# Token gathers of an expert-choice layer: two halves of eight experts, or eight pairs

## Chip, cores and metric

The kernel runs on one core of one Trainium2 chip. The metric is the time of one execution on the device, in microseconds (us). Three runs of the kernel before gave 1915.8, 1917.1 and 1922.41 us; their median is 1917.1 us.

## What is computed

The reference is a chain of two transformer blocks. The first has two layers (a gated linear attention with sparse attention, then pooling with stick-breaking attention, each with a gated feed-forward network). The second puts 16 meta tokens ahead of the 256 tokens (272 rows of 1024 features), runs differential attention and a convolution, and ends with the expert layer, which is the part that matters here:

```python
def expert_choice_ffn(h, w_router, w_gate, w_up, w_down):
    cap = EC_CAPACITY_FACTOR * L // N_EXPERTS        # 2 * 272 // 16 = 34
    def one_group(hs):
        aff = jax.nn.softmax(jnp.einsum('ld,de->le', hs, w_router), axis=-1)
        g, idx = lax.top_k(aff.T, cap)
        xg = hs[idx]
        a = jnp.einsum('ecd,edf->ecf', xg, w_gate)
        u = jnp.einsum('ecd,edf->ecf', xg, w_up)
        y = jnp.einsum('ecf,efd->ecd', jax.nn.silu(a) * u, w_down)
        y = y * g[..., None]
        return jnp.zeros((L, D)).at[idx.reshape(-1)].add(y.reshape(-1, D))
```

Each of 16 experts picks the 34 tokens with the highest affinity to it, runs them through gate, up and down matrices (1024 by 2048, 1024 by 2048, 2048 by 1024, all float32), and its weighted outputs are added back to the tokens' rows. Every expert has its own 24 MiB of weights, 384 MiB in all.

## The kernel before, in words

Every engine has a program of its own, written out by hand; all waits are on semaphores. The parts of the program follow one another: first layer, its feed-forward part, second layer, its feed-forward part, differential attention, experts (`pe_experts`, `act_experts`, `dve_experts`, `pool_experts`, and the tail of `sync_program`).

**Routing.** `pe_experts` multiplies by the router (line 919), turns the logits, the affinities and the tokens (lines 925, 940, 933), and counts the rank of each picked token (line 956). VectorE finds the picks with five rounds of eight maxima (lines 2067 and 2069), and writes the one-hot matrix `OH` (line 2089): for each token row, 16 experts by 34 places, a one where the token takes that place of that expert. It is written for experts 0 to 7 first, and then for 8 to 15, in three instructions each, one for each tile of token rows (128, 128 and 16 rows). The semaphore `onehot` counts them.

**Gather.** The tokens' rows are gathered by matmuls (line 969). The tokens `FT` are the stationary operand (128 features of one token tile), `OH` the moving one. For each of 8 feature chunks and each half of the experts, three matmuls (token tiles of 128, 128 and 16 rows) add up in one PSUM bank, 272 columns wide (8 experts by 34). ScalarE copies the odd chunks to `XG`, VectorE the even ones (line 2096). A float32 matmul stands as two MATMUL records and two LDWEIGHTS records in the trace, so the 24 matmuls of a half are 48 records. The first half is gathered in front of expert 0, the second in two portions of four chunks, behind the first gate/up step of experts 2 and 3.

**An expert.** Gate and up are done in four steps of 512 columns each (`gate_up(e, i)`, lines 990 and 991, 16 matmuls in a step; the gate uses the array's columns 0 to 33, and the up matmul beside it columns 64 to 97). ScalarE applies the silu (line 1473), VectorE multiplies (line 2104), TensorE turns the result (`turn_hidden`, line 1000), and four steps `down(e, i)` follow (lines 1011 and 1012). Behind `gate_up(e, 0)` other work is put: the gather portions at e = 2 and 3, two turns of the way back for each e from 1 to 4 (`back_map`, line 977), and at each even e from 2 the addition of the last pair of experts to the tokens (`combine`, line 1027).

**Weights.** SyncE starts all weight transfers in order, 2 MiB each, into a ring of five slots (`sp_weight`, line 2261). For each expert the order is g0 u0 g1 u1 g2 u2 g3 u3 d0 d1 d2 d3. A transfer into a slot is issued when the TensorE step that read the slot last has ended. `gate_up` frees two slots at its end, and `down` one. At the end of `gate_up(e, 0)` the transfers of g1, u1 and g2 have been issued already, and u2 and g3 follow; at the end of `gate_up(e, 1)` come u3 and d0. Expert 0 is different: its g0, u0, g1, u1 and g2 are loaded into the ring during the attention, and u2, g3 and u3 into places outside the ring (lines 2333 and 2339) during the routing. The next transfer, d0 of expert 0, needs the slots of `gate_up(0, 0)`.

**PSUM.** The eight banks are used in turn in the order of the TensorE program (`pe_bank`); a use waits until the last reader of the use before has taken it.

Of the kernel before, what the change touches and what calls it, by code (L numbers as in the profile page):

```python
# [16 lines left out]
KC = D // 128  # L17
# [7 lines left out]
E_N = 16  # L25
CAP = 2 * L // E_N
# [2 lines left out]
NHD = 6  # L29
MAGIC = 12582912.0  # L30
NP = 64 + CAP
LAM0 = 0.8 - 0.6 * math.exp(0.0)
TILES = ((0, 128), (128, 128), (256, 16))
SET_EXP, SET_SILU, SET_SIN = 6, 18, 9
# [370 lines left out]
def pe_bank(nc, k, key, takers=1, hold=False):  # L405
    u = k.banks.take(key, takers, hold)
    if u.before:
        nc.tensor.wait_ge(u.taken, u.before)
    return u
# [502 lines left out]
def pe_experts(nc, k):  # L912
    pe, s, v, P, ring = nc.tensor, k.sem, k.ex, k.banks, k.ring
    ident, ones = k.cc("ident"), k.cc("ones")
    u = pe_bank(nc, k, "router")
    pe.wait_ge(s["small"], 16)
    for c in range(KC):
        pe.wait_ge(s["hn"], HN["ffn2"] + c + 1)
        ins = pe.matmul(u.t[0:16, 0:L], k.WS[:, c, :], k.H[:, c, :], start=c == 0, stop=c == KC - 1)
    ins.then_inc(u.full, 1)  # L920
    u = pe_bank(nc, k, "route", takers=2)
    t = P["router"]
    pe.wait_ge(t.taken, t.done)
    for i, (r, m) in enumerate(TILES):
        ins = pe.transpose(u.v(3, 16)[0:m, i, :], v.LG[0:16, r:r + m], ident[0:16, 0:16])
# [11 lines left out]
    u = pe_bank(nc, k, "affinity")  # L937
    for i, (r, m) in enumerate(TILES):
        pe.wait_ge(s["raff"], 2 * i + 2)
        ins = pe.transpose(u.t[0:16, r:r + m], v.AFF[0:m, i, :], ident[0:m, 0:m])  # L940
# [3 lines left out]
    u = pe_bank(nc, k, "picked")  # L944
    pe.wait_ge(s["rtop"], 10)
    for i, (r, m) in enumerate(TILES):
        ins = pe.transpose(u.v(3, 16)[0:m, i, :], v.WK[0:16, 6 + r:6 + r + m], ident[0:16, 0:16])
    ins.then_inc(u.full, 1)
    u = pe_bank(nc, k, "rank")
    t = P["picked"]  # L950
    pe.wait_ge(t.taken, t.done)
    for i, (r, m) in enumerate(TILES):
        for j in range(i + 1):
            km = TILES[j][1]
            lt = k.cc("before")[0:km, 0:m] if j == i else ones[0:km, 0:m]
            ins = pe.matmul(u.v(3, 16)[0:m, i, :], lt, v.MSK[0:km, j, :], start=j == 0, stop=j == i)
    ins.then_inc(u.full, 1)
    for i in range(3):
        for half in range(2):
            t = P["tokens", i, half]  # L960
            pe.wait_ge(t.taken, t.done)
    hw = E_N * CAP // 2

    def gather(half, c):
        u = pe_bank(nc, k, ("gather", half, c))
        for i, (r, m) in enumerate(TILES):
            if c == 0:
                pe.wait_ge(s["onehot"], 3 * half + i + 1)
            ins = pe.matmul(u.t[:, 0:hw], v.FT[0:m, i, c * 128:(c + 1) * 128], v.OH[0:m, i, half * hw:(half + 1) * hw],  # L969
                            start=i == 0, stop=i == 2)  # L970
        ins.then_inc(u.full, 1)

    def back_map(g):
        u = pe_bank(nc, k, ("back", g))
# [5 lines left out]
    def gate_up(e, i):  # L980
        wg, wu = k.gate_up_at(e, i)
        u = pe_bank(nc, k, ("egu", e, i))
        pe.wait_ge(wg.sem, wg.n)
        pe.wait_ge(wu.sem, wu.n)
        for c in range(KC):
            if i == 0 and e % 8 == 0:
                t = P["gather", e // 8, c]
                pe.wait_ge(t.taken, t.done)
            xs = v.XG[:, c, e * CAP:(e + 1) * CAP]
            pe.matmul(u.t[0:CAP, :], xs, wg.v(KC, 512)[:, c, :], start=c == 0, stop=c == KC - 1)  # L990
            ins = pe.matmul(u.t[64:64 + CAP, :], xs, wu.v(KC, 512)[:, c, :], start=c == 0, stop=c == KC - 1)  # L991
        ins.then_inc(u.full, 1)
        wg.left = wu.left = (u.full, u.n)
# [32 lines left out]
                stat.upto(max(c - 3, 0))  # L1026
            pe.matmul(u.t[:, 0:L], v.Y[0:NP, g % 2, c * 128:(c + 1) * 128], v.OGT[0:NP, g, :], start=True, stop=True).then_inc(u.full, 1)  # L1027

    for c in range(KC):
        gather(0, c)  # L1030
    for e in range(E_N):
        gate_up(e, 0)
        if e in (2, 3):
            for c in range(4 * e - 8, 4 * e - 4):
                gather(1, c)
        if 1 <= e <= 4:
            back_map(2 * e - 2)
            back_map(2 * e - 1)
        if e and e % 2 == 0:
            combine(e // 2 - 1)  # L1040
        gate_up(e, 1)
        turn_hidden(e, 0)
        gate_up(e, 2)
        turn_hidden(e, 1)
        gate_up(e, 3)
        turn_hidden(e, 2)
        u = pe_bank(nc, k, ("eo", e), takers=2, hold=True)
        down(e, 0, u)
        turn_hidden(e, 3)
        for i in range(1, 4):  # L1050
            down(e, i, u)
        P.drop(("eo", e))
# [17 lines left out]
def act_table(nc, n):  # L1070
    nc.scalar.add_instruction(mybir.InstLoadActFuncSet(
        name=nc.get_next_instruction_name(), engine=mybir.EngineType.Activation, act_func_set_id=n, ins=[], outs=[]))


def act_out(nc, u, dst, src, f=ACT.Copy, **kw):

    nc.scalar.wait_ge(u.full, u.n)
    nc.scalar.activation(dst, src, f, **kw).then_inc(u.taken, 1)
# [365 lines left out]
def act_experts(nc, k):  # L1444
    act, s, v, P = nc.scalar, k.sem, k.ex, k.banks
    act_stat(nc, k, "ffn2", 0)
    act_out(nc, P["router"], v.LG[0:16, :], P["router"].t[0:16, 0:L])
    u = P["route"]
    act.wait_ge(u.taken, u.done - 1)
    for i, (r, m) in enumerate(TILES):  # L1450
        act.activation(v.AFF[0:m, i, :], u.v(3, 16)[0:m, i, :], ACT.Exp, bias=v.mx[0:m, i:i + 1],
                       accum_out=v.sm[0:m, i:i + 1]).then_inc(s["rexp"] if i < 2 else u.taken, 1)

    def turn_tokens(i):
        m = TILES[i][1]
        for half in range(2):
            act_out(nc, P["tokens", i, half], v.FT[0:m, i, half * 512:half * 512 + 512], P["tokens", i, half].t[0:m, :])

    for i in range(3):
        turn_tokens(i)  # L1460
    hw = E_N * CAP // 2

    def gather(half, c):
        if c % 2:
            act_out(nc, P["gather", half, c], v.XG[:, c, half * hw:(half + 1) * hw], P["gather", half, c].t[:, 0:hw])

    def gate(e, i):
        u = P["egu", e, i]
        act.wait_ge(u.full, u.n)
        if 4 * e + i >= 2:  # L1470
            t = P["egu", e, i - 2] if i >= 2 else P["egu", e - 1, i + 2]
            act.wait_ge(t.taken, t.done)
        act.activation(v.SG[0:CAP, i % 2, :], u.t[0:CAP, :], ACT.Silu).then_inc(s["esilu"], 1)  # L1473

    for c in range(KC):
        gather(0, c)
    act_table(nc, SET_SILU)
    for e in range(E_N):
        gate(e, 0)
        if e in (2, 3):  # L1480
            for c in range(4 * e - 8, 4 * e - 4):
                gather(1, c)
        if 1 <= e <= 4:
            for g in (2 * e - 2, 2 * e - 1):
                act_out(nc, P["back", g], v.OGT[0:NP, g, :], P["back", g].t[0:NP, 0:L])
        for i in range(1, 4):
            gate(e, i)
        u, g, r = P["eo", e], e // 2, 64 * (e % 2)
        act.wait_ge(u.full, u.n)
        if e == 0:  # L1490
            act.wait_ge(s["yzero"], 1)
        if g >= 2:
            t = P["comb", g - 2, KC - 1]
            act.wait_ge(t.full, t.n)
        act.activation(v.Y[r:r + CAP, g % 2, 0:512], u.t[0:CAP, :], ACT.Copy).then_inc(u.taken, 1)
        act.activation(v.Y[r:r + CAP, g % 2, 512:1024], u.t[64:64 + CAP, :], ACT.Copy).then_inc(u.taken, 1)
    for c in range(KC):
        act_square(nc, k, M, c, P["comb", 7, c])
    act_table(nc, SET_EXP)
    act_stat(nc, k, "fin", M)  # L1500
# [542 lines left out]
def dve_experts(nc, k):  # L2043
# [30 lines left out]
    t, u = u, P["rank"]  # L2074
    dve.wait_ge(u.full, u.n)
    dve.wait_ge(t.taken, t.done)
    for half in range(2):
        for i, (r, m) in enumerate(TILES):
            if not half:
                dve.scalar_tensor_tensor(out=v.SV[0:m, i, :], in0=u.v(3, 16)[0:m, i, :], scalar=1.0, in1=v.MSK[0:m, i, :],  # L2080
                                         op0=ALU.add, op1=ALU.mult).then_inc(s["rank"] if i < 2 else u.taken, 1)
                if i < 2:
                    dve.wait_ge(s["rank"], i + 1)
                else:
                    dve.wait_ge(u.taken, u.done)
            o = v.OH[0:m, i, half * 8 * CAP:(half + 1) * 8 * CAP].rearrange("p (e s) -> p e s", s=CAP)
            io = k.cc("iota")[0:m, :].rearrange("p (a s) -> p a s", a=1).to_broadcast([m, 8, CAP])
            sv = v.SV[0:m, i, 8 * half:8 * half + 8].rearrange("p (e a) -> p e a", a=1).to_broadcast([m, 8, CAP])
            dve.tensor_tensor(o, io, sv, ALU.is_equal).then_inc(s["onehot"], 1)
    hw = E_N * CAP // 2  # L2090

    def gather(half, c):
        if c % 2 == 0:
            u = P["gather", half, c]
            dve.wait_ge(u.full, u.n)
            dve.tensor_copy(v.XG[:, c, half * hw:(half + 1) * hw], u.t[:, 0:hw]).then_inc(u.taken, 1)

    def hidden(e, i):
        u, n = P["egu", e, i], 4 * e + i
# [20 lines left out]
                dve.wait_ge(t.taken, t.done)  # L2120
            dve_residual(nc, k, u, u.t[:, 0:L], c, 0, None)

    for c in range(KC):
        gather(0, c)
    for e in range(E_N):
        hidden(e, 0)
        if e in (2, 3):
            for c in range(4 * e - 8, 4 * e - 4):
                gather(1, c)
        if e and e % 2 == 0:  # L2130
            combine(e // 2 - 1)
        hidden(e, 1)
        turned(e, 0)
        hidden(e, 2)
        turned(e, 1)
        hidden(e, 3)
        turned(e, 2)
        turned(e, 3)
# [337 lines left out]
```

## Time and profile before

| | |
|---|---|
| median of 3 runs | 1917.1 us |
| the profiled execution, its own time | 1914.45 us |
| its span in the profile | 1912.8 us |
| TensorE busy | 1672.8 us (87%), 8723 matmul records |
| VectorE, ScalarE, GpSimd busy | 33%, 20%, 3% |
| moved by DMA | 577.30 MB, mean 302 GB/s |
| mean granted TensorE clock | 0.941 of full speed |
| chain that ended last | TensorE 67%, DMA 24%, VectorE 6% |
| gate/up matmuls of line 990 | 1008 records, busy 483.6 us; idle ahead of them 128.2 us, ended by the DMA of the up weights |

The routing ends and the gather begins 941 us after the start of the span; the experts run from 967 to 1896 us. A row of the stage table has the time window, its length, for each engine the busy us and the number of instructions, then the granted TensorE clock (1.00 is 2.4 GHz, 0.50 is 1.2 GHz), the busy share of the DMA engines and the rate in GB/s. A row of a timeline has start, duration from the start of the first to the end of the last instruction merged, engine, line, and in square brackets the idle time before it with what ended it.

### The profile page before, as it was taken

The page shows a single profiled execution, that of the slowest core. Times are in us where ns is not written, and L with a number is a line of the kernel's source. Part 1 is how long each engine was busy: PE and PEld are TensorE (multiplying, and loading weights), DVE is VectorE, ACT ScalarE, POOL GpSimd, SP SyncE. Part 2 cuts the span into 40 slices and gives each one's busy share as a digit, 9 for nine tenths or more (in the row PEclk, how much of TensorE's full clock was granted, in tenths as well). Part 3 has the DMA queues.
Part 4 walks back from the last instruction along what each step waited for, and adds up shares of the span by engine and source line. Part 5 has one row for each costly group of instructions (what it writes and reads, how often), then busy time and mean ns, then how long its engine had stood idle before and what let it go on. Part 6 is the DMA issues. An engine that isn't in the chain of part 4 may idle for free.

```text
span 1912.8 us, 20481 instructions
## 1 busy us (share of the span) xinstructions
PE 1672.8 (87%) x8723; PEld 998.9 (52%) x8723; DVE 634.1 (33%) x1218; ACT 378.8 (20%) x659; POOL 51.0 (3%) x47
## 2 busy tenths in 40 slices
PE   2998899999889998999798888978879788888787
PEld 1775799997679998767432322322223222222223
DVE  5567277745847554352310100101001010010102
ACT  3213344333333433141100000000000000000001
POOL 4101000000000000100010000000000000000000
PEclk7989999999989999999789999989999899899999
DMA  9554258646547445223459899999999999999995
GB/s 398 217 220 179 107 199 331 240 155 246 223 173 265 166 168 197 88 88 131 177 224 424 367 428 404 429 430 427 430 431 430 431 430 431 430 424 429 428 430 242
DMA packets 43740, 577.30 MB, mean 302 GB/s; under 512 B 4721, under 2 KB 6786, under 8 KB 7298
## 3 DMA queue, kind: packets, MB, share of 16 engines
q1 hardware_dynamic: 43650, 576.00, 73.4%
q8 instruction: 69, 1.13, 0.2%
q14 instruction: 21, 0.17, 0.0%
HBM read 574.93 MB, written 1.05 MB: 301 GB/s over the span
## 4 chain that ended last, share of the span: by engine, by line
PE 67%; DMA 24%; DVE 6%; ACT 2%; issue 1%; POOL 1%; SPq 0%; DVEq 0%; ACTq 0%
DMA RING_T<-in_w_up 22%; PE P L990 16%; PE P L419 13%; PE P L1011 6%; PE P L700 4%; PE P L701 4%; PE P L702 4%; PE P L428 3%; PE P L721 2%; PE P L720 2%; PE P L719 2%; PE P L969 2%; PE P L1027 2%; DVE RING_T L1565 1%; DMA RING_T<-in_ada_w 1%; PE P L446 1%
## 5 line engine op out<-in xcount | busy, mean ns | idle before, releaser
L990 PE MATMUL P<-RING_T,SCR 128*34 128x512 f32 x1008 | 483.6, 637 | 128.2 <-DMA RING_T<-in_w_up 128.1
L991 PE MATMUL P<-RING_T,SCR 128*34 128x512 f32 x992 | 477.5, 638 | 0.0
L990 PEld LDWEIGHTS P<-RING_T,SCR 128*34 128x34 f32 x1008 | 114.8, 119 | 444.2 <-issue 443.8
L2104 DVE TENSOR_TENSOR SCR<-P,SCR 34x512 f32<-34x512 f32 x64 | 44.4, 693 | 777.3 <-ACT SCR L1473 777.3
L1011 PE MATMUL P<-RING_T,SCR 128*34 128x512 f32 x512 | 228.4, 595 | 13.7 <-DMA RING_T<-in_w_down 13.7
L1012 PE MATMUL P<-RING_T,SCR 128*34 128x512 f32 x512 | 228.4, 594 | 0.0
L700 PE MATMUL P<-SCF 128*128 128x256 f32 x704 | 204.6, 291 | 15.8 <-DVE SCF L1837 10.9
L701 PE MATMUL P<-SCF 128*128 128x256 f32 x704 | 202.2, 287 | 0.0
L702 PE MATMUL P<-SCF 128*128 128x256 f32 x704 | 202.1, 287 | 0.0
L419 PE MATMUL P<-HWC,RING_T 128*128 128x256 f32 (+1 forms) x832 | 194.8, 392 | 7.9 <-ACT HWC L1111 4.1
L419 PEld LDWEIGHTS P<-HWC,RING_T 128*128 128x128 f32 x832 | 160.1, 194 | 40.1 <-issue 14.1
L1473 ACT ACTIVATE SCR<-P 34x512 f32<-34x512 f32 x64 | 37.9, 592 | 610.0 <-PE P L991 610.0
L700 PEld LDWEIGHTS P<-SCF 128*128 128x128 f32 x704 | 137.8, 196 | 18.0 <-issue 11.7
L701 PEld LDWEIGHTS P<-SCF 128*128 128x128 f32 x704 | 138.4, 197 | 0.0
L702 PEld LDWEIGHTS P<-SCF 128*128 128x128 f32 x704 | 138.3, 196 | 0.0
L1011 PEld LDWEIGHTS P<-RING_T,SCR 128*34 128x34 f32 x512 | 53.3, 111 | 158.3 <-issue 123.8
L1565 DVE SCALAR_TENSOR_TENSOR RING_T<-RING_T,CB 128x1024 f32<-128x1024 f32 x92 | 112.4, 1277 | 28.8 <-DMA RING_T<-in_ada_w 28.7
L1814 DVE TENSOR_TENSOR SCF<-RING_T,SCF 128x1024 fp32r<-128x1024 f32 x88 | 106.1, 1221 | 39.9 <-ACT SCF L1268 39.9
L991 PEld LDWEIGHTS P<-RING_T,SCR 128*34 128x34 f32 x992 | 113.2, 119 | 0.0
L1268 ACT ACTIVATE SCF<-RING_T 128x1024 fp32r<-128x1024 f32 x88 | 92.0, 1054 | 58.9 <-PE P L702 31.0
L719 PE MATMUL P<-SCF 128*128 128x256 f32 x352 | 100.4, 285 | 0.0
L720 PE MATMUL P<-SCF 128*128 128x256 f32 x352 | 99.6, 283 | 0.0
(247 smaller groups left out, 1748.4 us busy)
## 6 DMA issues: line engine op xcount, KB each, us to landing
RING_T<-in_w_down SPq DMA_DIRECT2D x64, 2048.0 KB, 12.6
RING_T<-in_w_gate SPq DMA_DIRECT2D x63, 2048.0 KB, 17.0
RING_T<-in_w_up SPq DMA_DIRECT2D x62, 2048.0 KB, 12.4
RING_T<-in_ada_w SPq DMA_DIRECT2D x24, 2048.0 KB, 10.4
RING_T<-in_ffn_w SPq DMA_DIRECT2D x22, 2048.0 KB, 8.4
RING_T<-in_ffn_w SPq DMA_DIRECT2D x22, 1024.0 KB, 4.8
RING_T<-in_ab_w_in SPq DMA_DIRECT2D x7, 2048.0 KB, 14.0
RING_T<-in_w_in SPq DMA_DIRECT2D x6, 2048.0 KB, 8.3
```

What stands on the lines that cost most here:

```text
L419: ins = nc.tensor.matmul(u.t[:, 0:n], wap[:, c, j * 128:(j + 1) * 128], h[:, c, :], start=c == 0, stop=c == KC - 1)
L700: pe.matmul(o, wh, v.HH[:, 0, c, :], start=c == 0, stop=False)
L701: pe.matmul(o, wh, v.HH[:, 1, c, :], start=False, stop=False)
L702: ins = pe.matmul(o, wl, v.HH[:, 0, c, :], start=False, stop=c == KC - 1)
L719: pe.matmul(o, wh, v.HR[:, f % NHD, 0, :], start=f == 0 and m % 2 == 0, stop=False, skip_group_check=True)
L720: pe.matmul(o, wh, v.HR[:, f % NHD, 1, :], start=False, stop=False, skip_group_check=True)
L990: pe.matmul(u.t[0:CAP, :], xs, wg.v(KC, 512)[:, c, :], start=c == 0, stop=c == KC - 1)
L991: ins = pe.matmul(u.t[64:64 + CAP, :], xs, wu.v(KC, 512)[:, c, :], start=c == 0, stop=c == KC - 1)
L1011: pe.matmul(u.t[0:CAP, :], hs, w.v(4, 1024)[:, c, 0:512], start=first, stop=end)
L1012: ins = pe.matmul(u.t[64:64 + CAP, :], hs, w.v(4, 1024)[:, c, 512:1024], start=first, stop=end)
L1565: nc.vector.scalar_tensor_tensor(out=src, in0=src, scalar=1.0, in1=k.CB[:, :], op0=ALU.mult, op1=ALU.mult, accum_out=k.MOD[:, layer, 4 * i ...
L1814: nc.vector.tensor_tensor(lo, w.up()[:, :, z, j * 128:(j + 1) * 128], hi.bitcast(F32), ALU.subtract).then_inc(k.sem["lo"], 1)
```

## The change

The experts' tokens are gathered for two experts at a time. A gather has 24 matmuls of 68 columns (2 by 34) in place of 272; four feature chunks share a PSUM bank, so that it needs two banks and two copies (features 0 to 511 by ScalarE, 512 to 1023 by VectorE). Gather 0 (experts 0 and 1) stands ahead of expert 0. Gather g + 1 stands behind `gate_up(e, 0)` of each odd expert e = 2g + 1 up to 13, ahead of `back_map` there. The one-hot matrix is written for experts 0 and 1 first and for the other 14 then. ScalarE's table load for the silu moves ahead of its copy of gather 0.

```diff
+PAIR = 2 * CAP
...
-    hw = E_N * CAP // 2
-
-    def gather(half, c):
-        u = pe_bank(nc, k, ("gather", half, c))
-        for i, (r, m) in enumerate(TILES):
-            if c == 0:
-                pe.wait_ge(s["onehot"], 3 * half + i + 1)
-            ins = pe.matmul(u.t[:, 0:hw], v.FT[0:m, i, c * 128:(c + 1) * 128], v.OH[0:m, i, half * hw:(half + 1) * hw],
-                            start=i == 0, stop=i == 2)
-        ins.then_inc(u.full, 1)
+    def gather(g):
+
+        for half in range(2):
+            u = pe_bank(nc, k, ("gather", g, half))
+            for c in range(4):
+                for i, (r, m) in enumerate(TILES):
+                    if half == 0 and c == 0:
+                        pe.wait_ge(s["onehot"], i + 1 if g == 0 else i + 4)
+                    ins = pe.matmul(u.v(4, PAIR)[:, c, :], v.FT[0:m, i, (4 * half + c) * 128:(4 * half + c + 1) * 128],
+                                    v.OH[0:m, i, g * PAIR:(g + 1) * PAIR], start=i == 0, stop=i == 2)
+            ins.then_inc(u.full, 1)
...
-            if i == 0 and e % 8 == 0:
-                t = P["gather", e // 8, c]
+            if i == 0 and e % 2 == 0 and c % 4 == 0:
+                t = P["gather", e // 2, c // 4]
                 pe.wait_ge(t.taken, t.done)
...
-    for c in range(KC):
-        gather(0, c)
+    gather(0)
     for e in range(E_N):
         gate_up(e, 0)
-        if e in (2, 3):
-            for c in range(4 * e - 8, 4 * e - 4):
-                gather(1, c)
+        if e % 2 and e < E_N - 1:
+            gather(e // 2 + 1)
         if 1 <= e <= 4:
             back_map(2 * e - 2)
             back_map(2 * e - 1)
...
@@ ScalarE
-    def gather(half, c):
-        if c % 2:
-            act_out(nc, P["gather", half, c], v.XG[:, c, half * hw:(half + 1) * hw], P["gather", half, c].t[:, 0:hw])
+
+    def gather(g):
+        act_out(nc, P["gather", g, 0], v.XG[:, 0:4, g * PAIR:(g + 1) * PAIR], P["gather", g, 0].v(4, PAIR))
...
-    for c in range(KC):
-        gather(0, c)
     act_table(nc, SET_SILU)
+    gather(0)
...
@@ VectorE
-    for half in range(2):
+
+    def gather(g):
+        u = P["gather", g, 1]
+        dve.wait_ge(u.full, u.n)
+        dve.tensor_copy(v.XG[:, 4:8, g * PAIR:(g + 1) * PAIR], u.v(4, PAIR)).then_inc(u.taken, 1)
+
+
+    for a, b in ((0, 2), (2, E_N)):
         for i, (r, m) in enumerate(TILES):
...
+            o = v.OH[0:m, i, a * CAP:b * CAP].rearrange("p (e s) -> p e s", s=CAP)
...
+    gather(0)
```

On ScalarE and VectorE the later gathers stand behind the first `gate` or `hidden` of the odd experts, as on TensorE.

## Rows read from the trace of the kernel before

**Rows 1.** Busy time by stage: first gather, first gate/up step, a stretch of experts

```profile
950.00:960.00 10.00, 10.00 (x19) 5.08 (x19) 0.89 (x2) 0.40 (x1) 0.00 (x0) 0.50 0.00 0
...
968.00:975.00 7.00, 7.00 (x26) 1.73 (x24) 0.00 (x0) 1.23 (x1) 0.00 (x0) 0.73 0.00 0
...
1200.00:1300.00 100.00, 87.45 (x402) 28.24 (x400) 11.48 (x24) 6.63 (x12) 0.00 (x0) 0.95 1.01 430
```

**Rows 2.** Timeline of TensorE's matmuls at the first gather

```profile
940.96 26.54 PE L969 MATMUL P<-SCR 128*128 128x272 f32 x48 [0.84 <-DVE SCR L2089]
967.43 1.07 PE L990 MATMUL P<-RING_T,SCR 128*34 128x512 f32 x1
```

**Rows 3.** Timeline of SyncE's transfers: the first after the gather, experts 5 and 13

```profile
976.68 7.67 SPq L2261 DMA_DIRECT2D RING_T<-in_w_down  x4
...
1264.16 0.33 SPq L2261 DMA_DIRECT2D RING_T<-in_w_up  x1
...
1734.36 0.33 SPq L2261 DMA_DIRECT2D RING_T<-in_w_up  x1
```

**Rows 4.** Timeline of weight loads in the gather behind expert 2's first step

```profile
1078.86 0.76 PEld L969 LDWEIGHTS P<-SCR 128*128 128x128 f32 x4 [0.84 <-issue]
1079.97 0.29 PEld L969 LDWEIGHTS P<-SCR 16*128 16x128 f32 x2 [0.36 <-issue]
1080.62 0.76 PEld L969 LDWEIGHTS P<-SCR 128*128 128x128 f32 x4 [0.36 <-issue]
```

**Rows 5.** Timeline of TensorE in the linear attention: short matmuls, then long ones

```profile
115.10 0.46 PE L598 MATMUL P<-SCR 128*128 128x128 f32 x2 [1.14 <-DVE SCR L1750]
115.49 0.43 PE L601 MATMUL P<-SCR 64*128 64x64 f32 x2
115.85 0.49 PE L598 MATMUL P<-SCR 128*128 128x128 f32 x2
...
125.95 5.06 PE L419 MATMUL P<-HWC,RING_T 128*128 128x256 f32 x16
```

**Rows 6.** Same stretch: window, us, TensorE busy, clock, DMA share, GB/s

```profile
118.00:120.00 2.00, 2.00 (x10) 0.61 1.02 434
...
128.00:130.00 2.00, 2.00 (x10) 0.83 0.00 0
```

**Rows 7.** Chain that ended last: start, us, what; experts 1, 2, 3, 5, 13

```profile
1028.02 12.38 DMA RING_T<-in_w_up
1040.53 1.04 PE P L990
...
1069.62 1.03 PE P L990
...
1078.93 7.06 PE P L969 x24
...
1097.89 8.05 DMA RING_T<-in_w_up
...
1135.28 1.03 PE P L990
...
1159.29 8.44 DMA RING_T<-in_w_up
...
1265.54 0.59 PE P L990
1272.64 12.16 DMA RING_T<-in_w_up
...
1734.75 0.59 PE P L990
```

**Rows 8.** Busy time by window where the transfers run dry, experts 2 and 3

```profile
1092.00:1094.00 2.00, 2.00 (x12) 0.59 (x10) 0.00 (x0) 0.00 (x0) 0.00 (x0) 1.00 0.16 66
...
1098.00:1100.00 2.00, 2.00 (x14) 0.72 (x14) 0.99 (x2) 0.49 (x1) 0.00 (x0) 1.00 0.71 147
...
1158.00:1160.00 2.00, 2.00 (x13) 0.59 (x11) 0.08 (x1) 0.59 (x1) 0.00 (x0) 1.00 0.14 57
```

More of the change, by code:

```diff
@@ L1460, in act_experts @@
         turn_tokens(i)
-    hw = E_N * CAP // 2
-    def gather(half, c):
-        if c % 2:
-            act_out(nc, P["gather", half, c], v.XG[:, c, half * hw:(half + 1) * hw], P["gather", half, c].t[:, 0:hw])
+    def gather(g):
+        act_out(nc, P["gather", g, 0], v.XG[:, 0:4, g * PAIR:(g + 1) * PAIR], P["gather", g, 0].v(4, PAIR))
     def gate(e, i):
@@ L1473, in gate @@
         act.activation(v.SG[0:CAP, i % 2, :], u.t[0:CAP, :], ACT.Silu).then_inc(s["esilu"], 1)
-    for c in range(KC):
-        gather(0, c)
     act_table(nc, SET_SILU)
+    gather(0)
     for e in range(E_N):
         gate(e, 0)
-        if e in (2, 3):
-            for c in range(4 * e - 8, 4 * e - 4):
-                gather(1, c)
+        if e % 2 and e < E_N - 1:
+            gather(e // 2 + 1)
         if 1 <= e <= 4:
@@ L2076, in dve_experts @@
     dve.wait_ge(t.taken, t.done)
-    for half in range(2):
+    def gather(g):
[3 more added lines that the diff above has]
+    for a, b in ((0, 2), (2, E_N)):
         for i, (r, m) in enumerate(TILES):
-            if not half:
+            if a == 0:
                 dve.scalar_tensor_tensor(out=v.SV[0:m, i, :], in0=u.v(3, 16)[0:m, i, :], scalar=1.0, in1=v.MSK[0:m, i, :],
@@ L2085, in dve_experts @@
                     dve.wait_ge(u.taken, u.done)
-            o = v.OH[0:m, i, half * 8 * CAP:(half + 1) * 8 * CAP].rearrange("p (e s) -> p e s", s=CAP)
-            io = k.cc("iota")[0:m, :].rearrange("p (a s) -> p a s", a=1).to_broadcast([m, 8, CAP])
-            sv = v.SV[0:m, i, 8 * half:8 * half + 8].rearrange("p (e a) -> p e a", a=1).to_broadcast([m, 8, CAP])
+            o = v.OH[0:m, i, a * CAP:b * CAP].rearrange("p (e s) -> p e s", s=CAP)
+            io = k.cc("iota")[0:m, :].rearrange("p (a s) -> p a s", a=1).to_broadcast([m, b - a, CAP])
+            sv = v.SV[0:m, i, a:b].rearrange("p (e a) -> p e a", a=1).to_broadcast([m, b - a, CAP])
             dve.tensor_tensor(o, io, sv, ALU.is_equal).then_inc(s["onehot"], 1)
[L2090 to L2096, printed above, removed]
+    gather(0)
     def hidden(e, i):
@@ L2121, in combine @@
             dve_residual(nc, k, u, u.t[:, 0:L], c, 0, None)
-    for c in range(KC):
-        gather(0, c)
     for e in range(E_N):
         hidden(e, 0)
-        if e in (2, 3):
-            for c in range(4 * e - 8, 4 * e - 4):
-                gather(1, c)
+        if e % 2 and e < E_N - 1:
+            gather(e // 2 + 1)
         if e and e % 2 == 0:
```

## The prediction

> **What bounds the kernel now.** I read the busy time by stage first. During a stretch of experts the transfers run without a gap at 430 GB/s while TensorE is busy 87% of it [rows 1]: there the DMA engines set the pace, and a transfer of 2 MiB takes 2.097 MB / 430 GB/s = 4.88 us. During the first gather it is the reverse: the DMA share is 0.00 [rows 1], since everything that has room is loaded. SyncE issues the next transfer at 976.68 us [rows 3], when the first gate/up step ends, and that step waits for the gather, 26.54 us from 940.96 to 967.43 us [rows 2]. So TensorE's gather lies wholly on the path, and what it gets shorter there, the whole chain of 184 later transfers starts earlier. TensorE's other work counts only where it leaves the transfers dry. The chain that ended last shows where that could be: behind expert 2's first step (start 1069.62) stands a gather portion of 7.06 us, and the second step ends at 1097.89 [rows 7]. The transfers run dry at about 1092.3 and return at about 1098.6 [rows 8]: some 6.3 us are lost. At expert 3 (1135.28 to 1159.29 [rows 7]) some 2 us are [rows 8].
>
> From these two I take a rule of thumb. If the time from the start of `gate_up(e, 0)`, which begins when u0 lands, to the end of `gate_up(e, 1)` is S, the loss is S - 22.0 us: 28.3 - 22.0 = 6.3 for expert 2, and 24.0 - 22.0 = 2.0 for expert 3. It is what three transfers underway and two issued at the end of the first step can cover (5 x 4.88 = 24.4 us, less some 1.6 us by which a landing is seen late, less some 0.7 us for the restart). Counted from the landing of u1, two transfers later, the limit is 22.0 - 9.75 = 12.25 us.
>
> **What 24 short matmuls cost.** Today a feature chunk, six records, takes 1.76 us at full clock [rows 4]. Each record streams 2 x 272 columns, 0.227 us at 2.4 GHz, 1.36 in all; the other 0.40 us are two changes between 128 and 16 token rows, at which the weight load is not hidden, 0.20 us each. The half-clock gather agrees: 26.54 / 8 = 3.32 us a chunk, 2.72 of it streams, 0.30 us a change [rows 2]. With 68 columns a record streams only 0.057 us (0.113 at half clock), so the loads of 128 columns set the pace. I take 0.107 us for one (2 cycles a column), which leaves 0.09 us of drain in a change. The nearest rows bear it out: L598 and L601 alternate every 0.75 us [rows 5], and my sum for that is 0.32 us of streams, 2 x 0.20 for changes and 0.05 for a load longer than its stream, 0.77. So a chunk costs 4 x 0.107 + 0.057 + 0.095 = 0.58 us for the two large tiles and 2 x 0.107 + 0.057 + 0.095 = 0.37 for the small one: 0.95 us, **7.6 us a gather at full clock**, and 13.4 us at half clock. Bounds: if every load but those of the changes were hidden, 24 x 0.113 + 16 x 0.20 = 5.9 us; if a matmul cost what it does with 272 columns, 24 x 0.588 = 14.1 us. The alternating stretch is nearer than either, so 7.6.
>
> **The first gather.** The clock is at half in this stretch (0.50) and stays there until about 4 us into the dense gate/up step [rows 1]; shorter matmuls give it no more reason to rise. Gather 0 takes 13.4 us in place of 26.5, and the narrower first compare lets it start 0.2 us earlier: **-13.35 us**, handed on to the transfers unshortened. The split of the one-hot matrix moves work of equal width behind the point where TensorE starts; it is over in some 3 us, before VectorE's copy of the second bank. ScalarE copies the first bank under the matmuls of the second, VectorE's copy is wanted only by chunk 4 of the gate/up step, and the table load falls into a time when ScalarE is idle. All of this costs nothing; if one copy were not covered it would be half a microsecond. Copies number 16 of 272 columns before and after. SyncE's order, GpSimd's work (it still needs six compares) and the bank turns stay as they are but for their numbering.
>
> **The second gather leaves experts 2 and 3.** At expert 2 S falls by 7.06 to 21.2, under 22.0: **-6.3 us**. Expert 3 loses its 7.06 and gets 7.6: **+0.5 us**.
>
> **The new gathers, if the clock held.** At experts 5 to 13 the first step ends shortly before u1 lands: 1264.16 against 1265.54, 1734.36 against 1734.75 [rows 3, 7]; the second step takes 1272.64 - 1265.54 = 7.1 us [rows 7]. A gather of 7.6 us is longer than that gap. Expert 5: 1264.16 + 7.6 + 7.1 = 1278.9, 13.3 us after the landing, loss 1.1 us; expert 13: 14.3, loss 2.1. The five (5, 7, 9, 11, 13) come to 1.1 + 2.1 + 1.6 + 1.1 + 2.1 = **+8.0 us**. Expert 1: its second step ends at 1028.02 and the transfer issued then lands at 1040.4 [rows 7], so what was ahead of it ended at 1040.4 - 4.88 - 1.6 = 1033.9; with the gather the step ends at 1035.6, restart 1036.3: **+2.4 us**. Sum: -13.35 - 6.3 + 0.5 + 8.0 + 2.4 = -8.75 us.
>
> **The clock.** I don't think it holds. In the alternating stretch TensorE was never idle, yet the granted clock fell: the window from 118 us shows 0.61, a fall at 118.4, 3.3 us after the first of these short matmuls, which had 1.1 us of idle ahead [rows 5, 6]. It came back in the window from 128 us (0.83), 2.7 us into the long matmuls that begin at 125.95 [rows 5, 6]; after the first gather it took 4.4 us (0.73 from 968 us) [rows 1]. There the array streamed 0.32 of every 0.75 us; in a gather of pairs it streams 0.34 of every 0.95 us, still less. The portions of 272 columns (1.36 of 1.76 us) kept the full clock. So I let it fall 4 us into each gather: the other 3.6 us become 3.6 x 13.4 / 7.6 = 6.35, +2.75 us; and the second step then starts at half clock for 4 us, +2.0 us. All seven experts are over their limit already, so each hands the 4.75 us on: **+33.3 us**.
>
> The Trainium skill (TensorE: Matmul & The Clock Gate, section "Why this matters for your kernels") warns of TensorE-idle gaps between bursts as what lowers the clock. A gather of pairs has no such gap; by that rule alone the clock would hold and the sum would be -8.75 us. The alternating stretch disagrees with taking idleness as the only cause: no idle time stands inside it.
>
> **Sum.** -8.75 + 33.3 = +24.5 us on 1914.45, 1939.0 us. The profiled execution lies 2.65 us under the median of the runs; on the median it is 1941.6, and I say 1941.
>
> **Rivals.**
> 1. The clock holds in the gathers (other side): the sum is -8.75 us, 1908 on the median. For it: the portions of 272 columns ran through 7.06 us at full speed [rows 4, 7]. Against it: rows 5 and 6. It decides at the place `gather(g)` behind the first step of odd experts: faster if each costs under about 3.1 us of dry transfers, the 21.65 us that the first gather and the dry times of experts 2 and 3 give up, over seven. Chance 0.14.
> 2. The loads are hidden better (5.9 us a gather), while the clock falls: 4 us + 1.9 x 1.77 = 7.4 us in place of 10.35, seven times 3 us less, +3.5 us; with the lower first gather (some 10 us at half clock) 0. 1917 to 1920. Against it: the 0.75 us of rows 5. Chance 0.05.
> 3. A matmul costs by its count, not its columns (14.1 us a gather; nothing won at first): 13.35 + 7 x 6.5 more than the forecast's -8.75, past 1967 even at full clock. Against it: rows 5. Chance 0.02.
> 4. The start isn't handed on, because the transfers of expert 0 are bounded otherwise: 13 us worse, 1955. TensorE works through expert 0 on loaded weights, so little speaks for it. Chance 0.03.
>
> The forecast keeps 0.76. Its own spread: the clock can fall 2.5 to 6 us into a gather and return 2.5 to 6 us into the step, about 1.5 us on each of seven, and the gather's price is good to 0.5 us: 1926 to 1957. To hold 8 in 10 the range takes in part of the rivals below: 1913 to 1958. A measurement tells this kernel from no change at about 0.3%, 5.8 us. Faster by more: rival 1, most of it (1908 is under 1911.3), 0.14. Within: the second rival and the edge of the first and of the forecast, 0.06. Slower: 0.80.
>
> **What the profile after would show.** Line 969 with 384 records in place of 96; the first gather about 13.4 us, the first transfer behind it issued near 963.3 us; later gathers 9 to 11 us, with the clock at 0.5 in their second half and in the first 4 us of the gate/up step behind them; dry transfers of 5 to 8 us at each odd expert from 1 to 13 and none at expert 2; the stage over near 1920 us. The prediction is wrong if the clock stays at 1.00 in these gathers, if a gather takes under 6 or over 12 us, or if the transfers go on without a gap while it runs.

## The result, and the profile after

The changed kernel is slower: 1951.5 us, median of five runs (1947.39 to 1953.24), against 1917.1; the ratio is 1.017 with a 95% interval of 1.0154 to 1.0185. Repeated in a later job it gave 1948.8 against 1917.0, ratio 1.016 (1.0134 to 1.0186). The profiled execution took 1947.39 us, its span is 1946.1.

The first gather and what follows it, on TensorE's timeline and on SyncE's:

```profile
944.13 1.82 PE L957 MATMUL P<-SCR,C 128*128 128x16 f32 x12 [0.51 <-DVE SCR L2069]
946.57 13.43 PE L971 MATMUL P<-SCR 128*128 128x68 f32 x48 [0.62 <-DVE SCR L2092]
959.93 1.07 PE L992 MATMUL P<-RING_T,SCR 128*34 128x512 f32 x1
...
969.12 7.67 SPq L2255 DMA_DIRECT2D RING_T<-in_w_down  x4
```

The gather takes 13.43 us where it took 26.54 [rows 2]. From its start to the first new transfer pass 22.55 us, where they were 35.72 [rows 2, 3]. So the 13 us were won, and handed on. The later gathers, as pieces of the chain that ended last, at experts 1, 3, 5, 7, 9, 11 and 13:

```profile
1012.24 10.95 PE P L971 x48
...
1140.46 9.83 PE P L971 x48
...
1268.74 8.77 PE P L971 x48
...
1392.03 9.08 PE P L971 x48
...
1515.28 9.34 PE P L971 x48
...
1638.20 9.35 PE P L971 x48
...
1761.17 9.44 PE P L971 x48
```

None takes the 7.6 us that were forecast for full clock. Windows of 2 us over the first of them and the gate/up step behind it show why (window, its length, each engine's busy us, granted clock, DMA share, GB/s):

```profile
1012.00:1014.00 2.00, 2.00 (x14) 1.62 (x12) 0.69 (x1) 0.59 (x1) 0.00 (x0) 1.00 0.98 418
1014.00:1016.00 2.00, 2.00 (x13) 1.66 (x13) 0.00 (x0) 0.00 (x0) 0.00 (x0) 0.84 0.98 418
1016.00:1018.00 2.00, 2.00 (x8) 1.73 (x8) 0.00 (x0) 0.40 (x1) 0.00 (x0) 0.50 1.05 451
...
1026.00:1028.00 2.00, 2.00 (x6) 0.38 (x4) 0.00 (x0) 0.00 (x0) 0.00 (x0) 0.50 0.10 41
1028.00:1030.00 2.00, 2.00 (x10) 0.57 (x8) 0.00 (x0) 0.00 (x0) 0.00 (x0) 0.75 0.00 0
1030.00:1032.00 2.00, 2.00 (x13) 0.46 (x8) 0.00 (x0) 0.00 (x0) 0.00 (x0) 1.00 0.00 0
1032.00:1034.00 2.00, 2.00 (x13) 0.53 (x10) 0.00 (x0) 0.07 (x1) 0.00 (x0) 1.00 0.00 0
1034.00:1036.00 2.00, 2.00 (x14) 0.71 (x15) 0.99 (x2) 0.52 (x1) 0.00 (x0) 1.00 0.64 147
```

TensorE is busy in every window, and yet the clock falls to 0.50 some 3 us into the gather (0.84 from 1014 us) and comes back only at 1029 us, 4 us into the second gate/up step. Meanwhile no slot is freed, and from 1026 to 1035 us next to nothing is transferred. The idle time of line 992 by the up weights is 104.3 us where line 990 had 128.2: TensorE waits less and its weights come later.

The ledger, from first gather to end. The start of the gather lies 5.6 us later than before, in code the change doesn't touch (below). From that start to the first transfer: -13.2 us. From the first transfer to the landing of the last (976.68 to 1891.4 before, 969.12 to 1924.6 after): 914.7 and 955.5 us, **+40.8**. The rest of the span is unchanged. 5.6 - 13.2 + 40.8 = 33.2, and the spans differ by 33.3. The 40.8 us are transfer time lost. Where the rate falls below 430 GB/s I call it a dip, and its size is the sum of 1 - rate / 430 GB/s over windows of 1 us. The dips behind the seven gathers are 10.0, 8.6, 7.4, 7.0, 6.1, 5.9 and 5.7 us, 50.7 in all (good to some 0.5 us each, by where one lets a dip end). Before there were two, 7.2 and 3.1 us by the same count; 50.7 - 10.3 = 40.4.

### The profile page after: what moved, and what is told of

Same layout as the page of the kernel before. It is cut to its first block, busy times and chain, and to the rows that moved or that the text cites. A ratio compares the mean times of both kernels' runs of the same rounds, so it can differ in the third digit from the quotient of the medians.

```text
span 1946.1 us, 21069 instructions
## 1 busy us (share of the span) xinstructions
PE 1726.8 (89%) x9011; PEld 1045.7 (54%) x9011; DVE 634.0 (33%) x1218; ACT 378.3 (19%) x659; POOL 50.9 (3%) x47
## 4 chain that ended last, share of the span: by engine, by line
PE 67%; DMA 22%; DVE 7%; ACT 2%; issue 1%; POOL 1%; SPq 0%; DVEq 0%; ACTq 0%
DMA RING_T<-in_w_up 19%; PE P L992 19%; PE P L420 13%; PE P L701 4%; PE P L702 4%; PE P L703 4%; PE P L971 4%; PE P L1013 3%; PE P L722 2%; PE P L721 2%; PE P L720 2%; PE P L429 2%; PE P L1029 2%; DMA RING_T<-in_w_down 2%; DMA RING_T<-in_ada_w 1%; DVE RING_T L1561 1%
## 5 line engine op out<-in xcount | busy, mean ns | idle before, releaser
L992 PE MATMUL P<-RING_T,SCR 128*34 128x512 f32 x1008 | 491.3, 645 | 104.3 <-DMA RING_T<-in_w_up 104.3
L993 PE MATMUL P<-RING_T,SCR 128*34 128x512 f32 x992 | 484.9, 646 | 0.0
L1013 PE MATMUL P<-RING_T,SCR 128*34 128x512 f32 x512 | 230.4, 598 | 16.2 <-DMA RING_T<-in_w_down 16.2
L1014 PE MATMUL P<-RING_T,SCR 128*34 128x512 f32 x512 | 230.4, 598 | 0.0
L420 PEld LDWEIGHTS P<-HWC,RING_T 128*128 128x128 f32 x832 | 161.1, 195 | 40.4 <-issue 14.1
```

Of the source, the lines that this page charges most:

```text
L420: ins = nc.tensor.matmul(u.t[:, 0:n], wap[:, c, j * 128:(j + 1) * 128], h[:, c, :], start=c == 0, stop=c == KC - 1)
L1013: pe.matmul(u.t[0:CAP, :], hs, w.v(4, 1024)[:, c, 0:512], start=first, stop=end)
L1014: ins = pe.matmul(u.t[64:64 + CAP, :], hs, w.v(4, 1024)[:, c, 512:1024], start=first, stop=end)
```

## The experiments

My theory: a gather of pairs costs (a) by the clock, which its short matmuls let fall, and (b) by its own length, but only because it stands between the end of the first gate/up step and that of the second, where the five ring slots run out. Rivals: the gathers cost their own TensorE time wherever they stand; or it is loads and changes, not the streams, that set clock and price.

**The same kernel again (a1).** No edit.

> The changed kernel once more, unaltered. Its first profile spent 5.8 us more than the kernel before ahead of the gather, in code that the change doesn't touch; the falls and rises of TensorE's clock there stood at other points. If that belongs to one execution, the gather starts at another time now (anywhere from 940 to 950 us). If it belongs to the program, it starts at 946.6 us again. Everything behind the gather's start should repeat: first gather 13.4 us, and seven times 5 to 9 us in which the transfers run dry, about 1950 us.

```profile
941.76 13.43 PE L971 MATMUL P<-SCR 128*128 128x68 f32 x48 [0.62 <-DVE SCR L2092]
```

The gather starts at 941.76 us, not 946.57: the 5.6 us belong to one execution. Everything behind repeats: 13.43 us, and seven dips of 9.3, 8.4, 7.8, 6.2, 5.9, 6.4 and 6.5 us. From the gather's start to the end of the span are 998.2 us (first profile 999.5; the kernel before 971.8). That is 26 to 28 us of change where the medians differ by 32 to 34. Both profiled executions were the fastest of their sets (1947.4 and 1941.4), so the rest lies in what these profiles don't show, and stays open.

**Wider gathers (a2).** Gathers 1 to 7 stream 128 columns, of which 68 are used.

```diff
+WIDE = 128
+def wide(g):
+    if g == 0:
+        return 0, PAIR
+    return min(g * PAIR, E_N * CAP - WIDE), WIDE
...
-                    ins = pe.matmul(u.v(4, PAIR)[:, c, :], v.FT[0:m, i, (4 * half + c) * 128:(4 * half + c + 1) * 128],
-                                    v.OH[0:m, i, g * PAIR:(g + 1) * PAIR], start=i == 0, stop=i == 2)
+                    a, w = wide(g)
+                    ins = pe.matmul(u.v(4, w)[:, c, :], v.FT[0:m, i, (4 * half + c) * 128:(4 * half + c + 1) * 128],
+                                    v.OH[0:m, i, a:a + w], start=i == 0, stop=i == 2)
```

> Gathers 1 to 7 stream 128 columns in place of 68 (all but 68 of them unused), same place, same count of matmuls and loads; gather 0 stays. At full clock a chunk would take 4 x 0.107 + 0.107 + 0.095 + 2 x 0.107 + 0.107 + 0.095 = 1.05 us, a gather 8.4 us in place of 7.6. My theory (the clock falls in the gathers because the array streams so little in them): with 0.64 of every 1.05 us streamed the clock holds, a gather takes 8.4 us and not 9 to 11, the step behind it starts at full clock, and the kernel gains about 7 x 3.5 = 25 us, 1926. Rival (the clock falls because of the 24 loads and changes, whatever is streamed): it falls again, each gather takes 0.8 to 1.5 us longer, 1957 to 1962.

Measured 1922.4 us, 1.0034 (1.0022 to 1.0046) of the kernel before. With nearly twice the columns the kernel is 26 us faster. The chain's rows for gathers 1 to 3, and the windows at expert 1 (window, length, TensorE busy, clock, DMA share, GB/s):

```profile
1008.82 8.44 PE P L979 x48
...
1132.19 8.44 PE P L979 x48
...
1255.17 8.44 PE P L979 x48
```

```profile
1012.00:1014.00 2.00, 2.00 (x12) 1.00 1.04 442
1014.00:1016.00 2.00, 2.00 (x13) 1.00 1.01 434
1016.00:1018.00 2.00, 2.00 (x13) 1.00 0.98 418
...
1022.00:1024.00 2.00, 2.00 (x12) 1.00 0.37 156
1024.00:1026.00 2.00, 2.00 (x12) 1.00 0.00 0
1026.00:1028.00 2.00, 2.00 (x12) 1.00 0.95 238
```

All seven take 8.44 us (forecast 8.4), the clock stays at 1.00 through each gather and the second step behind it, and the dip at expert 1 is 4.2 us in place of 10. This settles (a): count of matmuls, loads and changes are as before, only the streams are longer, and the clock holds. What is left over the kernel before is (b), seven dips of 2.9 to 5.8 us.

The dips of a2 also test the prediction's rule, that S - 22.0 us are lost, S being the time from the start of the first gate/up step to the end of the second. The chain at expert 5 (the wait for u0, the first matmul, the gather, the wait behind the second step):

```profile
1229.07 16.28 DMA RING_T<-in_w_up
1245.48 1.03 PE P L1000
...
1255.17 8.44 PE P L979 x48
...
1270.65 8.08 DMA RING_T<-in_w_up
```

S is 1270.65 - 1245.48 = 25.2 us, so 3.2 us should be lost; the dip is 4.6 us. It is the same at the experts from 3 to 13: the dips of a2 are 0.8 to 1.5 us larger than S - 22.0, those of the changed kernel 1.0 to 2.0 us, and the two of the kernel before some 1 us (7.2 and 3.1 against 6.3 and 2.0).

**Gathers moved (a3).** 68 columns; gathers 2 to 7 behind the last down step of an even expert.

```diff
         gate_up(e, 0)
-        if e % 2 and e < E_N - 1:
-            gather(e // 2 + 1)
+        if e == 1:
+            gather(1)
...
         P.drop(("eo", e))
+        if e % 2 == 0 and 2 <= e < E_N - 2:
+            gather(e // 2 + 1)
```

(ScalarE's and VectorE's copies move likewise.)

> Gathers 2 to 7 move: from behind the first gate/up step of experts 3, 5, 7, 9, 11 and 13 to behind the last down step of experts 2, 4, 6, 8, 10 and 12, where TensorE waits for the next weights anyway. Gather 1 stays behind the first step of expert 1. My theory (a gather costs only by the slots that it keeps from being freed between the first two steps): the transfers run dry at expert 1 alone, the shortfall of six gathers, 40.7 us of transfer time in the profile of the changed kernel, is gone, and about 1950 becomes 1909. The gathers themselves take 8 to 12 us there, and the next gate/up step starts up to 5 us late without a price. Rival (they cost their own time wherever they are, TensorE being 89% busy): 1940 to 1950.

Measured 1920.2 us, 1.0021 (1.0005 to 1.0036): 29 us better than the changed kernel measured with it, not the 41 that I expected. So the gathers don't cost their own time wherever they stand, and the rival falls. But experts 7, 9, 11 and 13 still show dips of 3.5, 2.5, 3.5 and 2.5 us. The chain and the windows ahead of expert 7 (columns as in a2):

```profile
1361.65 9.55 PE P L971 x48
1371.21 1.00 PE P L992
```

```profile
1366.00:1368.00 2.00, 2.00 (x10) 0.66 1.01 434
1368.00:1370.00 2.00, 2.00 (x9) 0.50 1.00 426
...
1378.00:1380.00 2.00, 2.00 (x12) 1.00 0.59 254
1380.00:1382.00 2.00, 2.00 (x12) 1.00 0.06 25
```

The clock falls here as well, and the first gate/up step starts late and at half clock; it ends at 1381.1 us, and from 1379.2 on nothing is underway. My rule looked only at the end of the second step. The first step has a limit of its own, by the same working: up to its end three transfers are all there is, 3 x 4.88 = 14.6 us less the same 2.3 us, so some 12.3 us after u0's landing (an estimate).

**Both (b1).** The moved gathers with 128 columns.

> The moved gathers of the run before (2 to 7 behind the last down step of an even expert, 1 behind the first step of expert 1), now streaming 128 columns. There the moved gathers of 68 columns took 8.7 to 10.5 us and let the next expert's first step start at half clock, and the transfers ran dry by 2.5 to 3.5 us at the end of that step in experts 7, 9, 11 and 13. Theory: the clock holds, each gather takes 8.44 us, the step starts at full clock, some 4 us earlier, and these four shortfalls (12 us) and half of the one at expert 1 (9.6 to 4.2 us) go: 1920 - 17 = 1903. Rival (a longer stream in a gather costs what it adds, 8.4 against 7.6 us each): 1920 to 1926.

Measured 1902.8 us, ratio 0.9916 (0.9895 to 0.9938): faster than the kernel before. The gather ahead of expert 7, and the windows of it and the step behind it:

```profile
1353.09 8.51 PE L979 MATMUL P<-SCR 128*128 128x128 f32 x48
```

```profile
1358.00:1360.00 2.00, 2.00 (x13) 1.00 0.97 418
1360.00:1362.00 2.00, 2.00 (x14) 1.00 1.07 459
1362.00:1364.00 2.00, 2.00 (x12) 1.00 1.00 426
...
1368.00:1370.00 2.00, 1.51 (x10) 1.00 0.99 426
```

The step runs at full clock right away, and the transfers go on. The sum 1920 - 17 came out to the microsecond, and that is luck: the interval is 4 us wide on either side, and from the gather's start to the end of the span the two profiles differ by 12.8 us (976.2 in a3, 963.4 here, where the profiled execution was the slowest of four).

**The kernel before with a held clock (a4).** Nine matmuls that nobody reads.

```diff
     turn_tokens(2)
+    u = pe_bank(nc, k, "warm", takers=0)
+    for n in range(7):
+        ins = pe.matmul(u.t[:, 0:L], ones, k.C[:, 0:L], start=True, stop=True)
+    ins.then_inc(u.full, 1)
     u = pe_bank(nc, k, "picked")
```

(and two more behind the rank matmuls)

> The kernel before with nine matmuls more, whose result nobody reads (272 columns, 0.45 us each at full clock), seven in TensorE's wait for VectorE's picks and two in its wait for the first one-hot tile. If the first gather is slow by its clock (26.5 us at half, 24 x 0.588 = 14.1 us at full), the clock stays at 1.00 through routing and gather, the gate/up step behind it takes 7 us in place of 9.2, and the kernel gains 12.4 + 2.2 = 14.6 us, 1902.5: as much as gathering one pair first won. If the matmuls don't hold the clock, nothing changes, 1917, or 1918 to 1919 where they delay the turns.

Measured 1903.6 us, 0.993 (0.9915 to 0.9945).

```profile
936.66 3.37 PE L946 MATMUL P<-C 128*128 128x272 f32 x14
...
941.37 1.15 PE L960 MATMUL P<-SCR,C 128*128 128x16 f32 x12 [0.51 <-DVE SCR L2081]
942.45 1.18 PE L964 MATMUL P<-C 128*128 128x272 f32 x4
943.47 14.09 PE L977 MATMUL P<-SCR 128*128 128x272 f32 x48
...
964.59 7.67 SPq L2269 DMA_DIRECT2D RING_T<-in_w_down  x4
```

The unchanged gather by halves takes 14.09 us in place of 26.54, as the 0.588 us a matmul said it would. So half of the first gather's cost was the clock and not the width. From the gather's start to the first transfer are 21.1 us, 14.6 less than before: nine matmuls in two waits, some 4.5 us, give a little more than the change's 13.2 us, and leave nothing to be gathered later but what was.

**The changed kernel with the same nine (b3).**

> The changed kernel (68 columns) with the nine unread matmuls ahead. Theory (the short gather itself lets the clock fall): the clock stands at 1.00 when gather 0 starts and falls 2.5 to 6 us into it; it takes 9 to 11 us in place of 13.43, the gate/up step still starts at half clock: 3 to 4 us won, about 1946. Rival (the clock falls in the later gathers for another reason than their short streams, the gate/up steps around them): gather 0 stays at 1.00 and takes 7.6 us, the step behind it 7.0: 8 us won, 1942.

Measured 1948.1 us, 1.0152 (1.0131 to 1.0172): no gain over a1 that can be told. The windows at its first gather, which starts at 942.8 us:

```profile
940.00:942.00 2.00, 1.49 (x16) 1.00 0.96 410
942.00:944.00 2.00, 2.00 (x12) 0.87 0.47 197
944.00:946.00 2.00, 2.00 (x9) 0.50 0.06 25
```

The clock stands at 1.00 when the 68 columns begin, and falls within 1 us; the gather takes 12.53 us, and from its start to the first transfer are 22.3 us, as in a1 (22.4). In a4, with the same matmuls ahead, 272 columns held it through 14 us. It fell sooner than the 2.5 to 6 us I had put down; the short rank matmuls (L961, 1.15 us) just ahead may count in, which wasn't tried.

**All together (b2).** b1 with the nine matmuls and a first gather of 128 columns.

```diff
-    if g == 0:
-        return 0, PAIR
...
-    for a, b in ((0, 2), (2, E_N)):
+    for a, b in ((0, 4), (4, E_N)):
```

> The same with the nine unread matmuls ahead of the gather, and gather 0 with 128 columns too (the first one-hot instructions cover four experts). Theory: gather 0 takes 8.44 us in place of 13.43, the first gate/up step 7.0 in place of 9.2: 7 us less than the kernel without them, 1896, the fastest so far. If the clock falls in gather 0 all the same, 1901 to 1903.

Measured 1893.0 us, 0.9864 (0.9848 to 0.9881), the fastest here.

```profile
941.03 8.24 PE P L985 x48
```

From the gather's start to the first transfer are now 15.3 us, where 22.5 were in b1 and 35.7 before.

**The halves, spread (b4).** a4, with the second half's chunks two at a time behind the last down step of experts 1 to 4.

```diff
-        if e in (2, 3):
-            for c in range(4 * e - 8, 4 * e - 4):
-                gather(1, c)
...
         P.drop(("eo", e))
+        if 1 <= e <= 4:
+            gather(1, 2 * e - 2)
+            gather(1, 2 * e - 1)
```

> The kernel before, by halves of eight experts, with the nine unread matmuls, and with the second half's eight chunks two at a time behind the last down step of experts 1 to 4, where TensorE waits for weights some 6 us, in place of four at a time behind the first step of experts 2 and 3. Two chunks take 3.5 us, so the next expert starts on time. Theory: the two dry times at experts 2 and 3 (6.4 and 2.4 us) go, 1903.6 - 9 = 1895. Rival: the dry time only moves, 1903.

Measured 1895.7 us, 0.988 (0.9859 to 0.9902), as forecast: the dry times of experts 2 and 3 go and don't come back elsewhere. Its interval overlaps that of b2, so pairs, cured of both their faults, are no more than level with halves treated the same way.

| kernel | median us | ratio to the kernel before | expected us |
|---|---|---|---|
| changed kernel (first job; a1) | 1951.5; 1948.8 | 1.017; 1.016 | 1941; 1950 |
| a2, 128 columns | 1922.4 | 1.0034 | 1926 |
| a3, moved | 1920.2 | 1.0021 | 1909 |
| a4, before with held clock | 1903.6 | 0.993 | 1902.5 |
| b1, moved and 128 columns | 1902.8 | 0.9916 | 1903 |
| b2, b1 with held clock | 1893.0 | 0.9864 | 1896 |
| b3, changed, nine matmuls ahead | 1948.1 | 1.0152 | 1946 |
| b4, halves spread, held clock | 1895.7 | 0.988 | 1895 |

## Why the prediction was right

By its steps, in the order of the text:

- *The first gather is on the path, the transfers' restart is handed on.* Right: -13.35 forecast; 13.43 us measured for the gather (13.4 forecast) and -13.2 us to the first transfer from its start, plus the 0.2 us of the narrower compare (TensorE idle 0.62 us ahead of the gather where it was 0.84).
- *Price of a short matmul: the weight loads set the pace.* Right. At half clock 13.43 against 13.4. The prediction doesn't show the sum behind 13.4; its terms with loads and streams doubled and the drain left at 0.09 us give 13.5. At full clock a2 took 8.44 against 8.4 for 128 columns. For 68 columns no gather ran wholly at full clock, but the mixed ones give it. At expert 5 the clock fell 6.0 us into the gather (0.89 in the window from 1274):

```profile
1274.00:1275.00 1.00, 1.00 (x7) 0.89 0.82 328
1275.00:1276.00 1.00, 1.00 (x4) 0.50 1.06 442
```

The other 2.7 us at half clock are 2.7 / 13.43 = 0.20 of a gather, so 6.0 us made 0.80 of one, 7.6 us for a whole (an estimate; at expert 1 the same working gives 7.5).

- *The clock falls in the later gathers.* Right, and the step that decided the sign: it fell in all seven, and held in all seven of a2. But it cost less than the 4.75 us apiece of the sum: it fell 3.1 us into the gather at expert 1 and 4.6 to 6.0 us into the others (4 forecast), and came back 2.5 to 4.1 us into the second step (4 forecast). The gathers took 8.8 to 11.0 us, 9.5 on average, where I had 10.35. The Trainium skill (TensorE: Matmul & The Clock Gate, "Why this matters for your kernels") warns of idle gaps between bursts of matmuls. Such gaps don't tell the changed kernel from a2: TensorE is busy throughout the gathers of both.
- *What it does to the transfers.* The span from first transfer to last landing grew by 40.8 us; the same terms of my sum (all but the first gather) are 37.85. The dips were larger than forecast at experts 1, 3 and 5 (10.0, 8.6 and 7.4 against 7.15, 7.25 and 5.85) and about as forecast at the last four (24.7 us together against 25.9), and expert 2's dip went as forecast. Expert 1's gather fell to half clock earliest, and its two turns of the way back ran at half clock too (1.56 us against 1.01), which the sum left out.
- *That these terms came out within 3 us is in part luck*: two of them were off and offset one another. With the clock held they were to be -6.3 + 0.5 + 8.0 + 2.4 = +4.6 us. In a2, which holds it, the part from the gather's start on is 977.4 us, 5.6 more than before; without the first gather's -13.2 that is +18.8, and with seven gathers 0.84 us shorter +13.0 (an estimate): **8 us more than forecast**. Most of it is the rule S - 22.0, which puts each dip 1 to 2 us too low, and there are five dips more than before. The clock then made 40.8 - 13.0 = 27.8 us, **5 us less than the 33.25 forecast**.
- *The total.* 24.5 us were forecast. Within the profiles the part from the gather on grew by 27.7 and 26.4 us; on the medians the difference is 34.4 and 31.8. So of the 7 to 10 us that the forecast lacks on the medians 2 to 3 are in its terms. The other 5 to 7 are not: the code ahead of the gather and the executions without a profile make them, and what they are is open.

Rival 1 needed the clock to hold, and it didn't. Had it held, its -8.75 us would have been too much: a2, with the clock held and gathers 0.84 us longer, took 1922.4 us; seven times 0.84 less are 1916.5 (an estimate from a2's rows; a gather of 7.6 us wasn't tried), no difference from the kernel before. Rivals 2 and 3 fall by the prices above, rival 4 by the first transfer. The limit on the second step, which the prediction used for all its dips, is one of two: the limit on the first didn't bind here, and it was a3's forecast that failed by it.

## What to carry to other kernels

Where transfers feed a ring, ask of moved work not whether its engine has room on average (TensorE was 87% busy) but which release of a slot it stands ahead of; moving six of the seven later gathers into a wait won 29 us. Splitting a matmul into narrower ones keeps the number of weight loads per piece: at 68 columns the loads set the pace (by the working that gave 13.4 and 8.4 us where 13.43 and 8.44 were measured), and each of the eight gathers pays for all 48 of them. And look at the granted clock of a slow stretch before restructuring it: here a few matmuls in an earlier wait gave all that the new order gave, without its price.

## What the runs showed of the hardware that I had not expected

A gather with more columns was the faster one. With 68 columns 24 matmuls took 8.8 to 11.0 us with the clock falling, with 128 columns 8.44 us each time with the clock at 1.00, and the gate/up step behind gained as well. And the clock depended on where it had stood: the 48 records of 272 columns stayed at 0.50 for 26.54 us when they began there, and at 1.00 for 14.09 us when nine matmuls had kept it up until then.

The part ahead of the gather isn't of equal length in each execution, though its code is the same. The router's matmuls, identical in all ten profiles but for the matmuls' line number, started between 923.4 us, in the kernel before, and 929.2 us, in the first profile after:

```profile
923.39 5.51 PE L919 MATMUL P<-HWC 128*16 128x272 f32 x16 [3.51 <-DVE HWC L1607]
```

```profile
929.22 5.51 PE L920 MATMUL P<-HWC 128*16 128x272 f32 x16 [3.51 <-DVE HWC L1603]
```

The other eight lie from 923.9 to 926.5. In the linear attention, for one, the clock stood at 0.50 from 118.4 to 128.7 us before [rows 6], and in the profile after from 117.7 us to past 130. So a few microseconds between two single profiles of such a kernel mean nothing; counting from a common event, as from the gather's start here, takes them out.
